# Where the vector engine's head steps stand in a prompt attention loop, and a sample output projection in column groups

## The reference

```python
def odd_layer(x, pos, ckv_past, kpe_past, norm_g, w_in, q_norm_g, kv_norm_g, w_q_b, w_uk, w_uv, w_out):
    z = rms_norm(x, norm_g) @ w_in
    c_q, c_kv, k_pe = jnp.split(z, [R_Q, R_Q + R_KV], axis=-1)
    q = (rms_norm(c_q, q_norm_g) @ w_q_b).reshape(B, T, H_C, D_NOPE + D_ROPE)   # 16 heads
    q_pe = rope(q[..., D_NOPE:], pos)
    ckv, kpe = rms_norm(c_kv, kv_norm_g), rope(k_pe, pos)
    # scores = (q . keys) * scale, causal for the prompt; p = softmax(scores); o = p @ values
    return x + o @ w_out, ckv, kpe
```

## Time and profile before

| what | value |
|---|---|
| median of 3 runs | 3587.05 us (3582.57 to 3587.59) |
| the profiled execution, its own time | 3615.96 us |
| its span in the trace | 3614.2 us |
| its mean granted clock | 0.956 |
| PE, DVE, ACT, POOL busy | 84%, 60%, 40%, 36% of the span |
| prompt attention loop | about 1764 to 1927 us of the span |
| sample attention block | about 1987 to 2256 us |

### The profile page before, as it was taken

The page is one execution under the profiler, slowest core; times in us unless marked ns, Lnnn a source line. Parts: engine busy times, 40 slices in busy tenths (PEclk is TensorE's granted clock), DMA queues, the critical chain, the costliest instruction groups (busy, mean ns, idle before and its releaser), DMA issues. The chain is left out here.

```text
span 3614.2 us, 33879 instructions
## 1 busy us (share of the span) xinstructions
PE 3043.4 (84%) x10529; PEld 1503.6 (42%) x10529; DVE 2184.8 (60%) x5215; ACT 1432.7 (40%) x4136; POOL 1297.4 (36%) x1112
## 2 busy tenths in 40 slices
PE   8987888888898888887889788788888889888886
PEld 6643334433344333424444664433433344433332
DVE  4863676667667767652342222667666766776764
ACT  2122444445444534442331222345444544544443
POOL 0211544444444444440000110344444444444442
PEclk9988999999999999998999788899999999999999
DMA  4016999999999999994100542999999999999998
GB/s 157 29 49 231 421 421 417 421 421 413 421 415 418 409 421 421 420 418 170 49 1 0 234 164 99 404 421 416 421 421 416 420 407 421 412 422 421 419 421 335
DMA packets 182961, 1194.51 MB, mean 331 GB/s; under 512 B 22815, under 2 KB 32831, under 8 KB 44789
## 3 DMA queue, kind: packets, MB, share of 16 engines
q0 software_dynamic: 154368, 1128.34, 75.4%
q1 hardware_dynamic: 27117, 63.11, 4.8%
q10 hardware_dynamic: 1296, 0.90, 0.1%
HBM read 1188.29 MB, written 4.46 MB: 330 GB/s over the span
## 5 line engine op out<-in xcount | busy, mean ns | idle before, releaser
L1439 PE MATMUL p_acc<-p_rows,p_diag 128*128 128x512 f32 (+1 forms) x4160 | 1979.6, 618 | 384.5 <-ACT p_diag L1131 383.1
L1280 DVE CUSTOM_DVE_ANT_0 p_rows<-p_rows,p_x_n 128x1024 f32<-128x1024 f32 x1024 | 1245.4, 1225 | 798.5 <-DMA p_rows<-in_peer_uv,p_ids 791.0
L1049 POOL DMA_INDIRECT p_rows<-in_peer_uv,p_ids x1024 | 1212.8, 1184 | 1392.9 <-PE p_acc L1439 1285.5
L1439 PEld LDWEIGHTS p_acc<-p_rows,p_diag 128*128 128x128 f32 (+1 forms) x4160 | 755.6, 193 | 1483.9 <-ACT p_diag L1131 761.4
L1125 ACT ACTIVATE p_acts<-p_dots 128x1 f32<-128x1 f32 x1040 | 208.3, 200 | 871.3 <-DVE p_dots L1280 869.6
L1131 ACT ACTIVATE p_diag<-ident,p_gated 128x128 f32<-128x128 f32 x1024 | 411.0, 401 | 33.5
L1127 ACT ACTIVATE p_gated<-p_acts,p_gates 128x1 f32<-128x1 f32 x1024 | 301.5, 294 | 33.2
L1388 PE MATMUL p_q_bank<-p_w_q,p_xT 128*128 128x256 f32 x1024 | 241.6, 391 | 20.4 <-issue 16.8
L1388 PEld LDWEIGHTS p_q_bank<-p_w_q,p_xT 128*128 128x128 f32 x1024 | 200.8, 197 | 75.9 <-issue 48.5
L1097 ACT COPY p_q_rows<-p_q_bank 128x256 f32<-128x256 f32 x68 | 25.3, 371 | 367.0 <-PE p_q_bank L1388 367.0
L2082 POOL MEMSET d_one<- 1x1 f32 x1 | 0.1, 89 | 334.9 <-POOLq L60 334.9
(11 more groups left out here) (382 smaller groups left out, 2509.1 us busy)
## 6 DMA issues: line engine op xcount, KB each, us to landing
p_rows<-in_peer_uv,p_ids POOLq DMA_INDIRECT x1024
p_w_q<-in_peer_w_q SPq DMA_DIRECT2D x16, 768.0 KB
a_w_in<-in_ab_w_in SPq DMA_DIRECT2D x6, 1024.0 KB
a_w_in<-in_ab_w_out SPq DMA_DIRECT2D x1, 4096.0 KB, 13.9
p_w_q<-in_peer_w_q SPq DMA_DIRECT2D x32, 128.0 KB, 3.7
c_arena<-in_c_w_out SPq DMA_DIRECT2D x1, 4096.0 KB, 12.7
d_past<-in_c_w_out SPq DMA_DIRECT2D x1, 4096.0 KB, 12.6
a_w_in<-in_ab_w_in SPq DMA_DIRECT2D x4, 1008.0 KB
```

What stands on the lines that cost most here:

```text
L1049: nc.gpsimd.indirect_dma_start(out=rows[:, slot % RING, :], out_offset=None, in_=w[f"peer_uv{layer}"], in_offset=bass.IndirectOffsetOnAxis ...
L1280: nc.vector.tensor_tensor_reduce(rows[:, k % RING, 0:D_MODEL], rows[:, k % RING, 0:D_MODEL], x, 1.0, 0.0, ALU.mult, ALU.add, dots[:, slot ...
L1439: last = nc.tensor.matmul(acc[done % 2][0:n, at], diag[:, slot // GROUP % 4, j, 0:n], rows[:, (slot + j) % RING, D_MODEL + 512 * b:D_MODEL ...
```

## The change

In the prompt's attention, `sm`, `low` and `sums` get a fourth buffer and `s_at` a fourth place, which is the second half of ps[1]. The queries lose that half: all heads use the first. TensorE runs the scores three units ahead. On VectorE `q_out(h + 2)` and `o_out(h // 2 - 1)` move to the end of unit t = 3. In the sample's tail the output projection is written as 64 passes of 256 columns in four column groups, four ScalarE copies gather the groups into a row, and VectorE adds it in two halves.

```diff
-        s_at = (ps[0][:, 0:512], ps[0][:, 512:1024], ps[2][:, 0:512])
+        s_at = (ps[0][:, 0:512], ps[0][:, 512:1024], ps[2][:, 0:512], ps[1][:, 512:1024])
...
             def exps(i):
                 act.wait_ge(max_ready, i + 1)
-                if i >= 3:
-                    act.wait_ge(p_ready, i - 2)
+                if i >= 4:
+                    act.wait_ge(p_ready, i - 3)
...
-                nc.vector.tensor_tensor(qT[:, h % 3, :], ps[1][:, 512 * (h % 2):512 * (h % 2) + 512], turn_q[:, h % 2, :], ALU.mult).then_inc(q_ready, 1)
+                nc.vector.tensor_tensor(qT[:, h % 3, :], ps[1][:, 0:512], turn_q[:, h % 2, :], ALU.mult).then_inc(q_ready, 1)
...
             def masked_max(i):
-                if i >= 3:
-                    dve.wait_ge(pT_ps, i - 2)
+                if i >= 4:
+                    dve.wait_ge(pT_ps, i - 3)
...
                 masked_max(i)
                 if i:
                     normed(i - 1)
-                if t == 1 and h + 2 < H_C:
+                if t == NT - 1 and h + 2 < H_C:
                     q_out(h + 2)
-                if t == 2 and h and h % 2 == 0:
+                if t == NT - 1 and h and h % 2 == 0:
                     o_out(h // 2 - 1)
...
             def queries(h):
-                else:
-                    pe.wait_ge(q_ready, h - 1)
+                if h:
+                    pe.wait_ge(q_ready, h)
                 for k in range(3):
-                    last = nc.tensor.matmul(ps[1][:, 512 * (h % 2):512 * (h % 2) + 512], w_qx[:, k, 128 * h:128 * h + 128], cqT[:, k, :], start=(k == 0), stop=(k == 2))
+                    last = nc.tensor.matmul(ps[1][:, 0:512], w_qx[:, k, 128 * h:128 * h + 128], cqT[:, k, :], start=(k == 0), stop=(k == 2))
...
             def scores(i):
-                else:
-                    pe.wait_ge(max_ready, i - 2)
+                elif i >= 4:
+                    pe.wait_ge(max_ready, i - 3)
...
             scores(0)
             scores(1)
+            scores(2)
             for i in range(NU):
                 h, t = divmod(i, NT)
-                if i + 2 < NU:
-                    scores(i + 2)
+                if i + 3 < NU:
+                    scores(i + 3)
                 turn_weights(i)
...
+            act.wait_ge(y_ps, 1)
+            for j in range(4):
+                nc.scalar.copy(y_row[:, 256 * j:256 * j + 256], turn[0][32 * j:32 * j + B, 0:256]).then_inc(y_rows, 1)
...
-            dve.wait_ge(y_ps, 1)
-            nc.vector.tensor_tensor(x_sb[0:B, NT, :], x_sb[0:B, NT, :], turn[0][0:B, :], ALU.add).then_inc(y_used, 1)
+            for n in range(2):
+                dve.wait_ge(y_rows, 2 * n + 2)
+                at = slice(512 * n, 512 * n + 512)
+                nc.vector.tensor_tensor(x_sb[0:B, NT, at], x_sb[0:B, NT, at], y_row[:, at], ALU.add).then_inc(y_used, 1)
...
-            for n in range(2):
-                for k in range(KC):
-                    last = nc.tensor.matmul(turn[0][0:B, 512 * n:512 * n + 512], oT[:, k, :], w_out[:, k, 512 * n:512 * n + 512], start=(k == 0), stop=(k == KC - 1))
+            for k in range(KC):
+                for j in range(4):
+                    last = nc.tensor.matmul(turn[0][32 * j:32 * j + B, 0:256], oT[:, k, :], w_out[:, k, 256 * j:256 * j + 256], start=(k == 0), stop=(k == KC - 1))
             last.then_inc(y_ps, 1)
```

More of the change, by code:

```diff
@@ L1517, in latent_projections @@
         qT = sb("qT", [128, 3, SEQ])
-        sm = sb("sm", [128, 3, SEQ])
+        sm = sb("sm", [128, 4, SEQ])
         junk = sm[:, :, :].rearrange("p b n -> p (b n)")
-        low = sb("low", [128, 3])
-        sums = sb("sums", [128, 3])
+        low = sb("low", [128, 4])
+        sums = sb("sums", [128, 4])
         pT = sb("pT", [128, 2, NT, SEQ])
         ps = [ctx.enter_context(nc.psum_tensor(f"c_ps{i}", [128, 1024], F32)) for i in range(4)]
-        s_at = (ps[0][:, 0:512], ps[0][:, 512:1024], ps[2][:, 0:512])
+        s_at = (ps[0][:, 0:512], ps[0][:, 512:1024], ps[2][:, 0:512], ps[1][:, 512:1024])
         pT_at = (ps[2][:, 512:1024], ps[3][:, 0:512])
@@ L1621, in exps @@
                 act.wait_ge(max_ready, i + 1)
-                if i >= 3:
-                    act.wait_ge(p_ready, i - 2)
+                if i >= 4:
+                    act.wait_ge(p_ready, i - 3)
                 keys = 128 * (i % NT + 1)
-                nc.scalar.activation(sm[:, i % 3, 0:keys], sm[:, i % 3, 0:keys], ACT.Exp, scale=-1.0, bias=low[:, i % 3:i % 3 + 1], accum_out=sums[:, i % 3:i % 3 + 1]).then_inc(e_ready, 1)
+                nc.scalar.activation(sm[:, i % 4, 0:keys], sm[:, i % 4, 0:keys], ACT.Exp, scale=-1.0, bias=low[:, i % 4:i % 4 + 1], accum_out=sums[:, i % 4:i % 4 + 1]).then_inc(e_ready, 1)
             def weights_out(i):
@@ L1734, in masked_max @@
                 dve.wait_ge(s_ps, i + 1)
-                if i >= 3:
-                    dve.wait_ge(pT_ps, i - 2)
-                nc.vector.tensor_tensor_reduce(sm[:, i % 3, 0:keys], s_at[i % 3][:, 0:keys], mask[:, SEQ - keys:SEQ], -MLA_SCALE, 3.0e38,
-                                               ALU.add, ALU.min, low[:, i % 3:i % 3 + 1]).then_inc(max_ready, 1)
+                if i >= 4:
+                    dve.wait_ge(pT_ps, i - 3)
+                nc.vector.tensor_tensor_reduce(sm[:, i % 4, 0:keys], s_at[i % 4][:, 0:keys], mask[:, SEQ - keys:SEQ], -MLA_SCALE, 3.0e38,
+                                               ALU.add, ALU.min, low[:, i % 4:i % 4 + 1]).then_inc(max_ready, 1)
             def normed(i):
@@ L1743, in normed @@
                 dve.wait_ge(e_ready, i + 1)
-                nc.vector.reciprocal(sums[:, i % 3:i % 3 + 1], sums[:, i % 3:i % 3 + 1]).then_inc(sum_inv, 1)
+                nc.vector.reciprocal(sums[:, i % 4:i % 4 + 1], sums[:, i % 4:i % 4 + 1]).then_inc(sum_inv, 1)
                 dve.wait_ge(sum_inv, i + 1)
-                nc.vector.tensor_scalar(sm[:, i % 3, 0:keys], sm[:, i % 3, 0:keys], sums[:, i % 3:i % 3 + 1], None, ALU.mult).then_inc(p_ready, 1)
+                nc.vector.tensor_scalar(sm[:, i % 4, 0:keys], sm[:, i % 4, 0:keys], sums[:, i % 4:i % 4 + 1], None, ALU.mult).then_inc(p_ready, 1)
             def o_out(a):
@@ L1884, in scores @@
                     pe.wait_ge(k_odd, 4)
-                else:
-                    pe.wait_ge(max_ready, i - 2)
+                elif i >= 4:
+                    pe.wait_ge(max_ready, i - 3)
                 keys = 128 * (t + 1)
-                nc.tensor.matmul(s_at[i % 3][:, 0:keys], qT[:, h % 3, cols_of(t)], kT[:, h, 0:keys], start=True, stop=True).then_inc(s_ps, 1)
+                nc.tensor.matmul(s_at[i % 4][:, 0:keys], qT[:, h % 3, cols_of(t)], kT[:, h, 0:keys], start=True, stop=True).then_inc(s_ps, 1)
             def turn_weights(i):
@@ L1894, in turn_weights @@
                 for b in range(i % NT + 1):
-                    last = nc.tensor.transpose(pT_at[i % 2][:, 128 * b:128 * b + 128], sm[:, i % 3, 128 * b:128 * b + 128], ident[:])
+                    last = nc.tensor.transpose(pT_at[i % 2][:, 128 * b:128 * b + 128], sm[:, i % 4, 128 * b:128 * b + 128], ident[:])
                 last.then_inc(pT_ps, 1)
@@ L2021, in latent_sample @@
         oT = sb("oT", [128, KC, B])
+        y_row = sb("y_row", [B, D_MODEL])
         turn = [ctx.enter_context(nc.psum_tensor(f"d_turn{i}", [128, 1024], F32)) for i in range(2)]
@@ L2044, in latent_sample @@
             "self_turn_ps", "self_pT_ready", "total_ps", "total_ready", "inv_ready", "o_ps", "o_used", "fold_ps", "olT_ready"))
-        oT_ps, oT_ready, y_ps, y_used = sem("oT_ps"), sem("oT_ready"), sem("y_ps"), sem("y_used")
+        oT_ps, oT_ready, y_ps, y_rows, y_used = sem("oT_ps"), sem("oT_ready"), sem("y_ps"), sem("y_rows"), sem("y_used")
         block = ctx.enter_context(nc.Block())
```

## The result

The changed kernel takes 3539.6 us (3532.9 to 3541.7, 4 runs) beside 3587.3 us (3582.6 to 3589.6, 4 runs) for the kernel before: ratio 0.9871 (0.9858 to 0.9884), 42 to 51 us less. In a second series it was 3541.1 us beside 3583.3: ratio 0.9891 (0.9877 to 0.9906), 34 to 44 us less. The forecast, 3547.5 us or a ratio of 0.9889, lies just above the first interval and inside the second. The measured 3539.6 us is near the low end of the forecast's range, 3538 to 3562. The profiled execution after took 3540.02 us, with a span of 3538.2.

A forecast was written before the change was run, and what follows sets the result against it. TensorE and VectorE wait for each other in turn in the prompt loop; the sample's tail overlaps nothing. From the 3587.05 us median, 30.5 (loop) and 9.0 (tail) come off: 3547.5 us, range about 3538 to 3562, chance 0.74.

The forecast's parts named there:

- The stream of a head: Prompt attention loop: TensorE's own work for one head in the new order takes 8.35 us, with no stall in odd heads.
- the even head: Prompt attention loop: a head with an o_out costs 8.57 us.
- the stall of 0.16 us at the named place: Even heads: the four turns wait 0.16 us for the scaling of 4h+3, queued on VectorE behind o_out and a maximum.
- The sum for the stretch: Loop from queries(2) to the weighted sum of head 14: 124.6 us instead of 156.8, 32.2 us less.
- the dip to 0.76 of the clock: Old loop's trace: lower clock over 7 us, worth 1.7 us; a run without it gains 30.5 us.
- 6.0 us of passes: Sample's output projection: 64 passes in four column groups take 6.0 us instead of 16.06, ends 3.66 and 6.7.
- The 1.1 us for copies and additions: Sample's tail: four copies and the second half addition take 2.32 us against 1.24 before, 1.1 us dearer.
- Net 9.0 forecast: Sample's tail: 10.1 us saved in passes less 1.1 added, net 9.0 us, between -1.1 and 11.3.
- A: Sample projection: column groups with 8 columns of weights do not overlap; gain 30.5 - 1.1, 3557.7 us. Chance 0.10.
- B: Prompt loop: another wait replaces the old, a 0.86 us stall per head stays; 3561.4 us. Chance 0.12.
- C: Both edits: no loop stall goes and the groups do not overlap; gain near zero, 3588 us. Chance 0.02.
- D: Prompt loop: denser TensorE stream gets the lower clock, making it slower; 3608 us at half share. Chance 0.02.

The follow-up runs named there:

- the last experiment: Changed kernel with o_out one unit later, behind the scaling of 4h+3, and column groups added straight from PSUM without copies: 3542.86 us beside 3541.05 for the changed kernel.
- the unchanged kernel again: The kernel before the change, traced again with no edit: 3612.32 us beside its 3612.86; a third look on another chip took 3614.35 us beside 3618.0.
- the loop alone: Only the prompt loop edit on the kernel before, sample tail as before: 3580.96 us beside 3612.86, ratio 0.9913.

## Why the prediction was right

**The new loop: right to 0.6 us.** The stream of a head was worked out at 8.35 us and measured 8.32; the even head at 8.57, measured 8.53, with the stall of 0.16 us at the named place and for the named reason, as the last experiment shows by removing it. The sum for the stretch was 124.6 us and it is 124.05 in three traces. The variants bear out the account: VectorE blocked in front of ready scores, by q_out in each head and by o_out in every second.

**The old loop: the step that was off.** I took the dip to 0.76 of the clock for chance and took its 1.7 us away for the median: "a run without it gains 30.5". Four traces of the old order (before, again twice, and with the new tail) have loops of 156.8, 158.6, 156.85 and 159.8 us. Without its dip the first would be 155.1, an estimate (156.8 less the 1.7). So all four have dips, 1.7 to 4.7 us of them, while none of eight traces with one of the edits in the loop shows one: their heads repeat to 0.01 us. In one of the four (the unchanged kernel again), columns as in the earlier trace rows:

```profile
1814.00:1820.00 6.00, 5.41 (x11) 2.07 (x9) 1.38 (x5) 1.40 (x5) 0.00 (x0) 0.79 0.00 0
...
1858.00:1864.00 6.00, 5.63 (x11) 2.10 (x10) 1.22 (x5) 1.27 (x4) 0.00 (x0) 0.76 0.00 0
```

In the traces the gain of the loop is therefore 32.8 to 35.7 us, not 30.5: the term that was mis-sized is the 1.7 us taken off for the dip. The median of the loop edit alone, 31.9 us less (26.7 to 36.5), can't confirm it. That the stalls themselves bring the dips is not shown. The kernel with only the third unit ahead stalls as long and has none, but it was run on the one chip where no old loop was traced. The kernel with only o_out moved, heads of 10.05 and 10.25 us, has none either, on a chip where the unchanged kernel has them. The Trainium skill (TensorE: Matmul & The Clock Gate, Part 1) says that activity releases the throttle and idling brings it back; the denser loops, with 1.00 throughout, agree; these two kernels, whose TensorE still stands in each head, are against it as the whole story.

**The tail: mechanism right, start of the clock unknown.** 6.0 us of passes, half the clock at first: where they did start so, they took 5.33. In the trace of after they began at full clock and took 3.64, the lower bound I had set. The 1.1 us for copies and additions was 1.07 (2176.44 to the end of the second addition at 2178.75 is 2.31, against 1.24). Net 9.0 forecast, 9.2 to 9.7 measured at equal clocks, 11.4 in the pair of traces. Full overlap held, or nearly: 64 passes in 3.64 us are sixteen groups of four at 0.23 us, where one pass of 256 columns takes 0.21; it is so with 8 columns of weights as with 32. The Trainium skill (TensorE: Matmul & The Clock Gate, Part 3) has three groups at 2.38 times the speed; the measurement decides, and here four groups gave 3.8 times (13.90 to 3.64).

**The profiled execution.** I noted that it stood 28.9 us above the median and went on. It was the sign that this trace had the long waits of the last section and the timed runs probably did not. It cost the forecast nothing, since the sum was a difference, but it would have misled anyone who compares the two traces stage by stage.

**The rivals.** A (groups of 8 columns do not overlap) falls by the 3.64 us. B (a wait in the old one's place) falls: the heads repeat at 8.32 and 8.53 us, with no stall but the 0.16. C falls with the loop alone. D is the reverse of what is seen: the denser stream kept the full clock, 1.00 over 130 us.

## What to carry to other kernels

Where two engines wait for each other in turn, look at what stands in the blocked engine's order behind the wait: a step that must wait for a long result belongs behind everything that is ready, just ahead of its own consumer's need. A deeper queue in front of the engine helps only after that (1.0 to 2.7 us lost alone, 6.9 won with the moves). Before two traces are compared, compare a stage that the change does not touch; if it differs by more than the gain, the traces are from unlike conditions.

## What the runs showed that was not expected

On two of the three chips of these experiments, VectorE stood 5 times for 5.3 to 5.5 us at the maximum over a sample's scores while GpSimd issued four gathers, and ScalarE's next copy came later with it; on the other chip and in the changed kernel's first trace the same wait was 2.1 us and ended with the scores. The sample block is 29 to 34 us longer there (249.7 against 215.9 to 220.7), and the whole kernel 29 to 35 us (3612.9 and 3618.0 against 3583.3).

The five waits are only half of it: 5 times 3.2 to 3.4 us more than 2.1 are 16 to 17. About 7 us more are lost at the block's start. There SyncE's transfer and ScalarE's copy wait for the same counter, which TensorE's last product (L2244, L2251 after) raises. In the trace of before that product starts late and both start 4.8 us after its recorded end, 2.6 us after the last of twelve gathers:

```profile
2002.97 0.38 PE L2244 MATMUL d_turn<-d_qnT,d_w_up 64*128 64x8 f32 x1 [1.02 <-issue]
...
2008.18 0.38 SPq L2076 DMA_DIRECT2D d_w_up<-in_c_w_uv  x1
2008.18 1.02 ACT L2104 COPY d_qlT<-d_turn 128x128 f32<-128x128 f32 x4 [15.89 <-remote]
```

In the trace of after they start at once, while GpSimd is still issuing gathers:

```profile
1961.31 7.01 PE L2251 MATMUL d_turn<-d_qnT,d_w_up 64*128 64x8 f32 x64 [1.15 <-DMA d_fold_h<-in_fold_h]
...
1968.34 0.38 SPq L2078 DMA_DIRECT2D d_w_up<-in_c_w_uv  x1
1968.35 1.02 ACT L2106 COPY d_qlT<-d_turn 128x128 f32<-128x128 f32 x4 [8.57 <-PE d_turn L2251]
```

So it is not VectorE alone that is held up. The Trainium skill (GPSIMD Engine Reference, Specifications) has GpSimd share its SBUF interfaces with VectorE, with contention for VectorE instructions in a 2-port perf mode or with two SBUF inputs. The maximum that waits here reads one tile, in PSUM, and TensorE, ScalarE and SyncE are late as well, so this case does not bear that out as the cause. What delays them, and why on some chips only, is open.
